# Where a conditioning product stands in a fused two-block kernel: five or six chunks in the convolution stage, and the order of the loads and low parts around them

## The reference

```python
def conv_module(h, w_pw1, w_dw, g_norm, w_pw2):
    a, b = jnp.split(h @ w_pw1, 2, axis=-1)
    u = depthwise_conv_31(a * jax.nn.sigmoid(b))
    return jax.nn.silu(rmsnorm(u, g_norm)) @ w_pw2

def mla(h, positions, w_a, g_q, g_kv, w_uq, w_ukv, w_o):
    a = h @ w_a                       # 512 query latents, 256 key latents, 64 rope
    # rmsnorm of both latents; queries by w_uq, keys and values by w_ukv;
    # rope, masked softmax over 8 heads, output by w_o
```

## Time and profile before

| | |
|---|---|
| median of 3 runs (lowest, highest) | 1797.1 us (1796.87, 1798.84) |
| the profiled execution's own time | 1796.37 us |
| its span, first to last instruction | 1794.6 us |
| TensorE, matmul / weight load | busy 1631.6 us (91%) / 1390.6 us (77%) |
| VectorE | busy 848.9 us (47%) |
| ScalarE | busy 678.8 us (38%) |
| HBM read | 425.13 MB, 237 GB/s over the span |
| mean granted TensorE clock | 0.966 of full speed |
| ffn0 / convolution stage / ffn1 begin on TensorE at | start / about 208 / 341 us |
| chain that ended last | PE 70%, DMA 21%, DVE 5%, ACT 2% |

### The profile page before, as it was taken

The page is one execution under the profiler, slowest core; times in us unless marked ns, Lnnn a source line. Parts: engine busy times, 40 slices in busy tenths (PEclk is TensorE's granted clock), DMA queues, the critical chain, the costliest instruction groups (busy, mean ns, idle before and its releaser), DMA issues.

```text
span 1794.6 us, 31776 instructions
## 1 busy us (share of the span) xinstructions
PE 1631.6 (91%) x13799; PEld 1390.6 (77%) x13799; DVE 848.9 (47%) x1159; ACT 678.8 (38%) x904; POOL 0.2 (0%) x4
## 2 busy tenths in 40 slices
PE   8999998999999999989999999999999866765765
PEld 7999985999999999879999988997785422422422
DVE  6555694755566655755665556974321000000001
ACT  5434543644444444544444456656412100100101
POOL 0000000000000000000000000000000000000000
PEclk9999999999999999999999999999999988888987
DMA  8755459555555555544655252435778999999997
GB/s 289 244 186 187 141 145 331 186 192 187 183 168 176 182 181 186 167 146 138 207 182 178 92 180 88 132 118 192 302 255 340 426 426 427 427 427 427 426 427 315
DMA packets 193518, 431.02 MB, mean 240 GB/s; under 512 B 8771, under 2 KB 150517, under 8 KB 178324
## 3 DMA queue, kind: packets, MB, share of 16 engines
q1 hardware_dynamic: 193428, 429.70, 66.0%
HBM read 425.13 MB, written 1.05 MB: 237 GB/s over the span
## 4 chain that ended last, share of the span: by engine, by line
PE 70%; DMA 21%; DVE 5%; ACT 2%; issue 1%; SPq 1%; DVEq 0%; ACTq 0%
PE banks L788 15%; PE banks L790 15%; PE banks L789 15%; DMA ring<-in_w_exp_down 3%; DMA xn<-in_w_exp_gate 3%; DMA arena<-in_w_exp_up 3%; DMA ring<-in_w_exp_up 3%; DMA squares<-in_w_exp_down 3%; DMA arena<-in_w_exp_gate 3%; DMA ring<-in_w_exp_gate 2%; PE banks L1237 2%; PE banks L1239 2%; PE banks L1238 2%; PE banks L1512 2%; PE banks L1382 2%; DMA h<-in_w_exp_up 2%
## 5 line engine op out<-in xcount | busy, mean ns | idle before, releaser
L2140 DVE TENSOR_TENSOR w_split<-ring,w_split 128x1024 fp32r<-128x1024 f32 x288 | 345.9, 1223 | 264.4 <-ACT w_split L1604 264.1
L788 PE MATMUL banks<-x_split,w_split 128*128 128x256 f32 x1600 | 457.4, 286 | 7.2 <-DVE w_split L2140 4.1
L790 PE MATMUL banks<-x_split,w_split 128*128 128x256 f32 x1600 | 453.4, 283 | 0.0
L789 PE MATMUL banks<-x_split,w_split 128*128 128x256 f32 x1600 | 453.3, 283 | 0.0
L1604 ACT ACTIVATE w_split<-ring 128x1024 fp32r<-128x1024 f32 x287 | 295.1, 1052 | 196.2 <-PE banks L790 184.0
L788 PEld LDWEIGHTS banks<-x_split,w_split 128*128 128x128 f32 x1600 | 307.8, 192 | 10.4 <-DVE x_split L2157 5.1
L789 PEld LDWEIGHTS banks<-x_split,w_split 128*128 128x128 f32 x1600 | 307.8, 192 | 0.4
L790 PEld LDWEIGHTS banks<-x_split,w_split 128*128 128x128 f32 x1600 | 307.7, 192 | 0.0
L788 PE MATMUL banks<-hid_split,w_split 128*128 128x256 f32 x704 | 199.6, 284 | 0.0
L789 PE MATMUL banks<-hid_split,w_split 128*128 128x256 f32 x704 | 199.2, 283 | 0.0
L790 PE MATMUL banks<-hid_split,w_split 128*128 128x256 f32 x704 | 199.2, 283 | 0.0
(11 more groups left out here) (484 smaller groups left out, 2296.2 us busy)
## 6 DMA issues: line engine op xcount, KB each, us to landing
ring<-in_ffn_w SPq DMA_DIRECT2D x131, 1024.0 KB, 5.3
arena<-in_w_exp_gate SPq DMA_DIRECT2D x13, 2048.0 KB, 45.3
ring<-in_w_mod SPq DMA_DIRECT2D x24, 1024.0 KB, 5.4
arena<-in_w_exp_down SPq DMA_DIRECT2D x12, 2048.0 KB, 44.9
arena<-in_w_exp_up SPq DMA_DIRECT2D x11, 2048.0 KB, 45.9
ring<-in_w_in SPq DMA_DIRECT2D x21, 1024.0 KB, 5.3
ring<-in_w_exp_down SPq DMA_DIRECT2D x9, 2048.0 KB, 44.1
ring<-in_w_exp_gate SPq DMA_DIRECT2D x7, 2048.0 KB, 45.9
```

Of the source, the lines that this page charges most:

```text
L788: mm(out_, hi, moving(0), start=start, stop=False, **kw)
L789: mm(out_, hi, moving(1), start=False, stop=False, **kw)
L790: return mm(out_, lo, moving(0), start=False, stop=stop, **kw)
L2140: ins = dve.tensor_tensor(half_part(n, o, 1), half_slot(n, o, columns), half_part(n, o, 0).bitcast(F32), ALU.subtract)
```

## The change

Four things are edited. (1) The stream has `mod_conv` with 10 slots and a new entry `mod_gap` with 2 slots between pw2 and ffn1, `MOD_EARLY` is 5, and chunk 5's product is made by TensorE between pw2 and ffn1. It is copied by ScalarE in ffn1's `start_products`, turned in the second mixer beside chunk 6, and taken by VectorE with it. TensorE waits for that copy before ffn1's loop, because its bank is used there. VectorE makes the second low part of ffn1's slot 0 after the update instead of before it. (2) SP asks for chunks 0 and 1, then shift 1, chunk 2, shifts 2 and 3, chunks 3 and 4, pw2, chunk 5. (3) On ScalarE the high parts of pw2's slot 0 stand before the copy of chunk 3. (4) In the second mixer chunk 7's product stands before the sum of the key latents' squares, VectorE makes uq 2's low part before the angles, and the four low parts of mla_o 1 and 2 are made one in each of the turns 2 to 5.

```diff
--- before.py
+++ after.py
@@ -51,7 +51,7 @@
 ROUNDS = len(LEVELS) + 2
 
 
-STREAM = [("ffn0", 33), ("pw1", 8), ("mod_conv", 12), ("pw2", 4), ("ffn1", 33), ("ffn2", 33),
+STREAM = [("ffn0", 33), ("pw1", 8), ("mod_conv", 10), ("pw2", 4), ("mod_gap", 2), ("ffn1", 33), ("ffn2", 33),
           ("mod_mla", 2), ("mla_a", 4), ("mod_latent", 2), ("uq", 4), ("ukv", 2), ("mod_rope", 2), ("mla_o", 4),
           ("ffn3", 33), ("mod_final", 2), ("w_in", 25), ("branch", 4), ("w_out", 4), ("experts", 12 * EXPERTS)]
 FIRST = {}
@@ -114,9 +114,9 @@
 
 
 
-MOD_CHUNKS, MOD_EARLY = 12, 6
+MOD_CHUNKS, MOD_EARLY = 12, 5
 MOD_SLOT = [FIRST["mod_conv"] + 2 * _c for _c in range(MOD_EARLY)] + \
-           [FIRST["mod_mla"], FIRST["mod_latent"], FIRST["mod_rope"], FIRST["mod_final"],
+           [FIRST["mod_gap"], FIRST["mod_mla"], FIRST["mod_latent"], FIRST["mod_rope"], FIRST["mod_final"],
             FIRST["w_in"] + 18, FIRST["w_in"] + 21]
 
 
@@ -675,12 +675,17 @@
                                      conv_pair(p)[32 * g:32 * g + 32, :, first:first + WIDE]
                                      ).then_inc(sem(f"pair_shifted_{p}"), 16)
 
-            for c in range(MOD_EARLY):
-                mod_chunk(c)
-                if c < 3:
-                    shift_pair(c + 1)
+            mod_chunk(0)
+            mod_chunk(1)
+            shift_pair(1)
+            mod_chunk(2)
+            shift_pair(2)
+            shift_pair(3)
+            mod_chunk(3)
+            mod_chunk(4)
             for j in range(4):
                 cols(FIRST["pw2"] + j, conv_w_pw2[0], 256 * j, 256, KD)
+            mod_chunk(5)
             ffn(1)
             ffn(2)
             mod_chunk(6)
@@ -883,6 +888,8 @@
                     norm_sums()
                 up(n0 + 1, 6, 0, between=norm_sums if f == 0 else None)
                 pe.wait_ge(sem("std_ready"), NORM[f"ffn{f}"])
+                if f == 1:
+                    pe.wait_ge(sem("mod_copied"), 6)
                 with pe.Fori(0, FF_STEPS // 2) as i:
                     for j in range(2):
                         n = n0 + 2 + 3 * j
@@ -994,7 +1001,6 @@
             pe.wait_ge(sem("squares_ready"), SQ_BEFORE["context"] + 1)
             sum_squares("conv_out", KD, T, 7)
             early_mod(4)
-            early_mod(5)
             sum_squares("context", KD, T, 4, at=T)
             pe.wait_ge(sem("mod_copied"), 5)
             for _ in range(KEEP_WARM):
@@ -1006,6 +1012,7 @@
                     turn_mod(MOD_EARLY - 1, mod_rows, 4, T + 8 * (MOD_EARLY - 1))
 
             pe.wait_ge(sem("mod_ready"), 2)
+            mod_product(5, cond_pad, 5)
             ffn(1)
             ffn(2)
 
@@ -1039,7 +1046,8 @@
                         sum_squares("mla_q", 4, T, 4)
                 done(last)
                 if j == 0:
-                    turn_mod(6, mod_rows_late, 7, 0)
+                    turn_mod(5, mod_rows_late, 7, 0)
+                    turn_mod(6, mod_rows_late, 7, 8)
             wait_part("mla_a", 3, 0)
             hi, lo = mla_hi("mla_a", 3, 0), mla_place("mla_a", 3, ring_r)
             for k in range(KD):
@@ -1047,9 +1055,9 @@
                     last = mm(ps[:, 3, 0:T], w[:, k].rearrange("p a c -> p (a c)"), mla_x[:, part, k, :],
                               start=(k == 0 and w is hi and part == 0), stop=(k == KD - 1 and w is lo))
             done(last)
+            mod_product(7, cond_late, 5)
             pe.wait_ge(sem("mod_taken"), 1)
             sum_squares("mla_kv", 2, T, 7, 4)
-            mod_product(7, cond_late, 5)
             pe.wait_ge(sem("xn_ready"), XN["mla_q"])
             wait_x("mla_q")
             for j in range(4):
@@ -1607,13 +1615,21 @@
                 for o in range(2):
                     split_hi(n, o, columns)
 
+            def mod_copy(c, rows, bank):
+                wait_done(act, MOD_SLOT[c] + 1)
+                if c >= 2 and c != 6:
+                    act.wait_ge(sem("mod_turned"), c - 1)
+                fn(rows[:, c % 2, :], ps[:, bank, :], ACT.Copy).then_inc(sem("mod_copied"), 1)
+
             def start_products(n0, gain, updates, norm, bank):
 
 
                 if n0 not in (FIRST["ffn0"], FIRST["ffn1"]):
                     split_hi_slot(n0)
-                if n0 - 1 in HALF:
-                    wait_done(act, n0 - 1 if n0 - 1 == FIRST["pw2"] + 3 else n0 - 2)
+                if n0 == FIRST["ffn1"]:
+                    wait_done(act, FIRST["pw2"] + 3)
+                elif n0 - 1 in HALF:
+                    wait_done(act, n0 - 2)
                 for k in range(KD):
                     if n0 == FIRST["ffn0"]:
                         if k % 2 == 0:
@@ -1635,6 +1651,8 @@
                     act.wait_ge(sem("h_loaded"), 4)
                 square(h[:, :, :], 0, T)
                 split_hi(n0 + 1, 1)
+                if n0 == FIRST["ffn1"]:
+                    mod_copy(5, mod_rows_late, 5)
                 if n0 != FIRST["pw1"]:
                     split_hi(n0 + 2, 0)
                 root(norm, bank, D)
@@ -1714,12 +1732,6 @@
                 act.wait_ge(sem("pe_mark"), PE_MARK[f"taps_summed_{pair}"])
                 fn(conv_acc[:, 2 * pair:2 * pair + 2, :], ps[:, PAIR_BANK[pair], :].rearrange("p (a t) -> p a t", t=T),
                    ACT.Copy).then_inc(sem("taps_copied"), 1)
-
-            def mod_copy(c, rows, bank):
-                wait_done(act, MOD_SLOT[c] + 1)
-                if c >= 2:
-                    act.wait_ge(sem("mod_turned"), c - 1)
-                fn(rows[:, c % 2, :], ps[:, bank, :], ACT.Copy).then_inc(sem("mod_copied"), 1)
 
             def square_pair(pair):
 
@@ -1743,8 +1755,8 @@
             square_pair(0)
             take_taps(3)
             square_pair(3)
+            split_hi_slot(FIRST["pw2"])
             mod_copy(3, mod_rows, 6)
-            split_hi_slot(FIRST["pw2"])
             root("conv_out", 7, D)
             mod_copy(4, mod_rows, 5)
             for g in range(4):
@@ -1754,7 +1766,6 @@
                 fn(x_g, x_g, ACT.Silu).then_inc(sem("x_hi"), 1)
             root("context", 4, D, region=T)
             split_hi_slot(FIRST["pw2"] + 1)
-            mod_copy(5, mod_rows, 6)
             split_hi_slot(FIRST["pw2"] + 2)
             split_hi_slot(FIRST["pw2"] + 3)
             act.wait_ge(sem("floor_logits"), 1)
@@ -2175,9 +2186,9 @@
                     for piece in range(0 if los_last else 3, 4):
                         lo(piece)
 
-            def mla_weights(name, j):
-
-                for o in range(MLA_PARTS[name, j]):
+            def mla_weights(name, j, parts=(0, 1)):
+
+                for o in parts[:MLA_PARTS[name, j]]:
                     dve.wait_ge(sem("w_hi_ready"), MLA_BEFORE[name, j] + o + 1)
                     dve.tensor_tensor(mla_part(mla_place(name, j, ring_r), name, j, o),
                                       mla_part(mla_place(name, j, ring), name, j, o), mla_hi(name, j, o).bitcast(F32),
@@ -2402,8 +2413,9 @@
             dve.wait_ge(sem("mod_ready"), 2)
             dve.wait_ge(sem("ctx_copied"), 1)
             normed("context", xn[:, :, 0:T], xn[:, :, 0:T], gain_mod[:, 1, :], region=T, rooted=True)
-            split_lo_slot(FIRST["ffn1"])
+            split_lo(FIRST["ffn1"], 0)
             update(1.0, ("ffn1", gains("ffn_norm2", 0)), FIRST["pw2"], los_last=True)
+            split_lo(FIRST["ffn1"], 1)
             ffn(1, after_slot=FIRST["ffn2"], after=("ffn2", gains("ffn_norm1", 1)))
             ffn(2, after_slot=FIRST["mla_a"], after=("mla", gains("mix_norm", 1)), rows=mla_x)
 
@@ -2418,7 +2430,7 @@
             dve.tensor_tensor(squares[:, 0:2, 0:T], squares[:, 0:2, 0:T], squares[:, 2:4, 0:T], ALU.add
                               ).then_inc(sem("squares_added"), 1)
             mla_weights("mla_a", 2)
-            mod_take(6, 1, 7, 0).then_inc(sem("mod_taken"), 1)
+            mod_take(5, 2, 7, 0).then_inc(sem("mod_taken"), 1)
             root("mla")
             latent_ps = banks(0, 3).rearrange("p (k t) -> p k t", t=T)
 
@@ -2449,6 +2461,7 @@
             latent_rest("mla_kv", 4, 6)
             mla_weights("ukv", 0)
             mod_take(7, 1, 4, T).then_inc(sem("mod_taken"), 1)
+            mla_weights("uq", 2)
             dve.wait_ge(sem("small_in"), 16 * 7)
             step(dve.tensor_copy(pos_f, pos_i[:, :]))
             settle()
@@ -2468,7 +2481,6 @@
             settle()
             step(dve.tensor_scalar(turns, turns, PI_LIMIT, -PI_LIMIT, ALU.min, ALU.max))
             dve.tensor_scalar(ang, ang, PI_LIMIT, -PI_LIMIT, ALU.min, ALU.max).then_inc(sem("angles_ready"), 1)
-            mla_weights("uq", 2)
             mla_weights("uq", 3)
             mla_weights("ukv", 1)
             step(dve.memset(rope_k, 0.0))
@@ -2523,8 +2535,8 @@
                     mod_take(8, 1, 7, 0).then_inc(sem("mod_taken"), 1)
                 if i >= 3:
                     mla_take(i - 3)
-                if 1 <= i <= 4 and i % 2 == 0:
-                    mla_weights("mla_o", i // 2)
+                if 2 <= i <= 5:
```

(1 more changed line is left out.)

## The result

The changed kernel took 1783.5 us in the median of 4 runs (1782.3 to 1785.24), against 1796.98 for the kernel before beside it (4 runs, 1796.59 to 1798.84): ratio 0.9924, 95% interval 0.9908 to 0.994. The profiled execution took 1782.3 with a span of 1780.5, 14.1 less than before. The median is the predicted one. The parts of the sum are not all as predicted; errors of opposite sign cancel, so that the agreement to a tenth is luck.

A forecast was written before the change was run, and what follows sets the result against it. Taken as bounds: the experts' weight transfers at the end, TensorE before that, apart from a few holes. 9.4 - 0.3 + 4.5 = 13.6 off 1796.4 gives 1782.8, with 0.7 to the median 1783.5 us; 8-in-10 range 1780.5 to 1788.5.

The forecast's parts named there:

- a stretch at 0.50 near 300: Sign against the forecast: TensorE's clock at its lower level (1.2 GHz) around 300 us, in the convolution stage.
- The landing of pw2's slot 0: Convolution stage: with 4 transfers ahead instead of 6, pw2's first weights land at 296.3 instead of 304.10, 7.8 us earlier.
- L: Time at which pw2's slot 0 weights land, said to set the convolution stage: 304.10 before, 296.3 forecast.
- Rival C: Convolution stage: early transfers cost the shifts what they save, only 2 MB leaving count; 11.3 us saved in all, chance 0.11.
- What hangs on L: Convolution stage: pw2's products begin at L + 9.1 = 305.4 instead of 314.82; 9.4 us saved (6.9 to 9.8).
- so I take full clock: Convolution stage: TensorE's wait before the turn shrinks from 4.9 to about 1 us, so the clock stays up; 1.6 saved.
- rival B: Both waits: the clock falls again although they are short; costs 1.6 + 1.3, 10.7 us saved in all, chance 0.17.
- The seam: Between pw2 and ffn1: chunk 5's product fills a wait of 1.68, small delays remain; 0.3 us lost (0 to 1.5).
- rival E: Between pw2 and ffn1: chunk 5's loads land after 329.9 instead of near 311; slower from 343 on, chance 0.03.
- The second mixer: Added turn costs 0.8, filled wait returns 0.7, no wait or slow clock at uq 2 (3.26, 1.3); 4.5 us saved.
- rival D: Second mixer: the wait moves to uq 3, whose low part has 1 us to spare; 9.1 saved in all, chance 0.08.
- the loop: Second mixer's multi-head loop: making mla_o's low parts one by one changes 0 (0.6 us gained to 0.6 lost).

The follow-up runs named there:

- e4: The changed kernel with the SP queue back in the old order, still five chunks in the convolution stage: 1784.78 us, ratio 0.9931 to the kernel before.
- e1: The changed kernel with the second mixer's three edits taken back: 1791.69 us, ratio 0.9963 to the kernel before.
- e11: The changed kernel run again unaltered: 1782.85 us, ratio 0.9929 to the kernel before.
- e9: The changed kernel with four chunks in the convolution stage instead of five, chunk 4 also loaded behind pw2: 1783.89 us, ratio 0.9933 to the kernel before.
- e2: The kernel before with the second mixer's three edits alone: 1790.86 us, ratio 0.9962 to the kernel before.
- e8: The changed kernel with the low parts of mla_o 1 and 2 made in pairs again: 1785.08 us, ratio 0.9934 to the kernel before.
- e3: The kernel before with the new SP queue order alone, still six chunks in the convolution stage: 1795.9 us, ratio 0.9991 to the kernel before.
- e6: The changed kernel with ten products of zeros in TensorE's wait ahead of chunk 3's turn: 1783.08 us, ratio 0.992 to the kernel before.
- e13: The changed kernel with chunk 3 copied before pw2's slot 0 is split, and 16 more zero products in the warm-up: 1782.62 us, ratio 0.9925.
- e12: e9 with chunk 2's turn behind the sum of the convolution's squares and five more zero products in the warm-up: 1780.64 us, ratio 0.9911.

## Why the prediction was right

The path was the right one: the landing of pw2's first slot sets the convolution stage, and the place of uq 2's low part sets the wait in the second mixer. By the prediction's own signs one step failed: TensorE waited 2.45 us where about 1 was reckoned, and a stretch at 0.50 near 300, named as a sign of being wrong, was there from 301.8 on. It cost little in this profile, and what was lost there was made up elsewhere.

*The landing of pw2's slot 0.* Right in mechanism, 1.0 too large. The queue was free at 279.69 (predicted 279.7) and L came at 297.30, not 296.3. The eight kernels with five chunks and the new order have L at 90.5 in the mean (89.9 to 90.8), so 6.3 was the typical gain, against 7.8 in the prediction. What was mis-sized is the pace: I took 11.2 for the four behind the first, 2.80 each, below the 2.96 that the row of the same queue gave, because the tail of shift 3 would be gone from the first of them. They took 12.27: 3.78, 2.71, 2.77, and 3.01 for pw2's own slot. Shift 3 stands right ahead of these transfers in the new order as well, and the long first gap was 3.71 in the kernel before: whatever makes it, it was not gone. pw2's slots landed 3.0 apart in the kernel before too. The stretch now moves 365 GB/s and not 384. Rival C, that only the two missing transfers count, is close: they made 5.1 of it (e4), the order the rest. No run moves chunk 1 alone, so what filling the idle stretch is worth by itself is not shown beyond that: at most the order's 1.2 to 1.8.

*What hangs on L.* The copy was ready at L + 2.6, as predicted. TensorE waited 2.45 instead of about 1, because L was 1.0 later and TensorE 0.5 earlier at that point. The step that failed is "so I take full clock": the stretch at 0.50 was there (rival B), but it cost only 0.2, since x's first low part is ready no earlier than L + 9.0 and lets the products begin at L + 9.24. Of the 1.6 for the clock 1.3 were won (L + 10.72 to L + 9.43), not by the absence of a slow stretch: 0.4 are the earlier copy, the rest is the turn, which ran at full clock. That the stretch was short enough is luck, as e1 shows. The lower bound of this term is mis-added besides: L = 297.9 with the clock as before gives 6.2 saved and not 6.9. Products at 306.73 against 305.4: 8.1 saved for 9.4. The rule of the Trainium skill that I set beside it (TensorE: Matmul & The Clock Gate, Part 1: The HAM clock gate), that the same code meets the gate differently from run to run, is borne out by e11 against the changed kernel.

What the prediction takes as given is that x must come behind L. It does so only by the order of two engines: ScalarE has the root, and VectorE the reciprocal and the normalization, behind the parts of pw2's slot 0. In the changed kernel the root's sum ended at 295.62, and ScalarE then stood until 297.38 for the landing; in e9, where the split was done before that sum ended, products began 6.4 behind the start of the root. With the root and x ahead of the slot's parts the products could begin some 2 to 5 us earlier, an estimate from these rows. No kernel tried it.

*The seam.* 0.3 lost was predicted, nothing was: from the first product of pw2 to the first of ffn1 it is 26.2 in both kernels, since chunk 5's 1.92 stood in place of the wait of 1.68 and the products of pw2 themselves took 24.3 instead of 24.5. The later second low part shows as 0.1 to 0.2 in ffn1. Chunk 5's slots landed at 309.02 and 311.74 for a product at 330.92: rival E had 19 us of room, as reckoned.

*The second mixer.* The turn cost 0.9 (e1 against before, 224.2 to 223.3; 0.8 predicted), the filled wait gave 1.1 (e2 against before; 0.7 predicted), uq gave 4.5 (3.26 and 1.3 predicted, together 4.56). uq 3 did not wait, though its low part was ready only 0.06 ahead: rival D missed by that much; the prediction had given it 1.0. The size in which this term was too small is the loop: 0 predicted, 0.6 gained (e8).

*The sum.* 8.1 - 0.15 + 0.1 + 4.5 + 0.6 = 13.2 up to ffn3, for 13.6; 0.9 came between ffn3 and the end, which I had not predicted and no edit touches. That stretch took 945.5 to 947.8 in the fourteen profiles, which are alike from there on, so it is taken for scatter and not for gain. In the traces the convolution stage with the seam gave 1.1 less than predicted, the second mixer 0.7 more, and the end 0.9 more: these cancelled. By medians the convolution half was worth 6.0 where 8.3 was predicted (9.4 less 0.3 and less the turn's 0.8), and the mixer half 6.9 where 5.3 was; both predictions lie within the intervals (4.3 to 9.3 at the widest), so the medians show neither error.

## What to carry to other kernels

Where one transfer's landing sets a stage, count the transfers that stand ahead of it in its queue and price each by its own row of that queue; filling an idle stretch further up helped here by 1.2 to 1.8, two transfers fewer in the count by 5.1. Ask also whether what waits for the landing must stand behind it on its engine. A wait that can't be removed should be laid where the work behind it has slack against another engine, because the granted clock may fall behind it: moving one copy on ScalarE, with no engine doing more or less, was worth 2.4 in the profiled execution. A chance at the clock is no term for a sum: price the place at either level and keep both ends.

## What the runs showed that was not expected

The fall of the clock does not go by the length of TensorE's wait alone. In the two stages it fell in or behind every wait from 3.04 (e8) to 4.9 us (before, e2, e3), ten in all. Of the shorter ones it fell in or behind 1.07 (e6), 2.09 (e9), 2.17 (e4), 2.45 (changed) and 2.75 (e1), and did not behind 2.88 (e11), 1.90 (e4), 1.68 (before, e2, e3), 1.14 (e11, ahead of pw2's products), 1.06 (e13) and 0.48 (e12). It fell behind 24 turning products (128x2, two columns each) in 2.79 us without any wait (e12), and not behind the same 24 in e9. What stood ahead of the fall in e6 was a wait of 1.07 and a turn of 1.05. What decides it is open: the same code fell in one profile and not in another (changed and e11).

Once fallen, it stayed at 0.50 for 3.4, 6.8 to 6.9 or 10.2 us. The runs of e13, whose profile shows no such stretch in these two stages, lie 0.8 us apart; those of the other eleven kernels 1.5 to 7, e11's 2.5, though its profile shows none either. That the clock makes this spread is not shown, since only one run of each has a profile.
